# Stored sums instead of local ones for half 1 of a feed-forward product made with seven multiplications

## What is computed

```python
h = _rmsnorm(x, ln2_w[l])
u = jax.nn.relu(jnp.einsum("bsd,df->bsf", h, w_ff1[l]))
x = x + jnp.einsum("bsf,fd->bsd", jnp.square(u), w_ff2[l])
```

## Time and profile before

| | us |
|---|---|
| median of 3 runs | 1502.23 (1501.88 to 1502.95) |
| the profiled execution | 1503.15 |
| its span (first to last instruction) | 1501.3 |
| PE busy in the span | 1494.2 |
| half 0: first product / second product | 178.8 / 162.4 |
| half 1: first product / second product, to the end | 178.3 / 166.4 |

### The profile page before, as it was taken

One profiled execution on the slowest core, in us unless ns is written; L12 is line 12 of the kernel. 1 busy time (PEld: TensorE's weight loads), 2 busy tenths in 40 slices (PEclk: granted clock), 3 DMA queues, 4 the chain that ended last, 5 costly groups with the idle time before them and its releaser, 6 DMA issues.

```text
span 1501.3 us, 19534 instructions
## 1 busy us (share of the span) xinstructions
PE 1494.2 (100%) x7450; PEld 1257.9 (84%) x7450; DVE 1143.3 (76%) x1362; ACT 811.1 (54%) x925; POOL 130.9 (9%) x169
## 2 busy tenths in 40 slices
PE   9999999999999999999999999999999999999999
PEld 7888888888888888888888888888888888888877
DVE  6877756878787877876666777778988566578978
ACT  6555444676664544544444544456655445466654
POOL 6000000000041100100000111110000111110000
PEclk9999999999999999999999999999999999999999
DMA  8878897745545444446799888766877656666874
GB/s 293 216 256 294 302 341 264 241 159 169 171 166 168 141 140 162 144 142 205 268 320 326 268 287 293 244 224 221 302 261 265 193 188 195 191 222 217 311 283 149
DMA packets 156889, 345.37 MB, mean 230 GB/s; under 512 B 8336, under 2 KB 8848, under 8 KB 153488
## 3 DMA queue, kind: packets, MB, share of 16 engines
q1 hardware_dynamic: 148960, 317.09, 62.9%
q0 software_dynamic: 6592, 25.17, 4.7%
q10 hardware_dynamic: 1264, 2.13, 0.4%
HBM read 317.11 MB, written 27.26 MB: 229 GB/s over the span
## 4 chain that ended last, share of the span: by engine, by line
PE 93%; DVE 3%; DMA 2%; ACT 0%; issue 0%; SPq 0%; ACTq 0%; DVEq 0%
PE banks L630 46%; PE banks L1006 16%; PE banks L1052 9%; PE banks L1009 8%; PE banks L1074 6%; DVE lo L2192 2%; DMA raw<-in_w_ff 2%; PE banks L646 1%; DVE t_sums L2223 1%; PE banks L903 1%; PE banks L912 1%; DMA raw<-w_sums 0%; PE banks L788 0%; PE banks L764 0%; PE banks L667 0%
## 5 line engine op out<-in xcount | busy, mean ns | idle before, releaser
L1574 DVE TENSOR_TENSOR lo<-raw,hi 128x1024 fp32r<-128x1024 f32 x383 | 472.0, 1237 | 251.1 <-ACT hi L1107 249.9
L1107 ACT ACTIVATE hi<-raw 128x1024 fp32r<-128x1024 f32 x383 | 404.5, 1059 | 444.0 <-PE banks L630 263.5
L630 PE MATMUL banks<-hi,st 128*128 128x512 f32 x1584 | 499.1, 396 | 0.0
L630 PEld LDWEIGHTS banks<-hi,st 128*128 128x128 f32 x1584 | 290.6, 189 | 55.8 <-DVE lo L1574 0.7
L1006 PE MATMUL banks<-st,hi 128*128 128x512 f32 x1024 | 321.6, 395 | 0.0
L630 PE MATMUL banks<-lo,st 128*128 128x512 f32 x792 | 309.4, 391 | 0.0
L1009 PEld LDWEIGHTS banks<-st,lo 128*128 128x128 f32 x1024 | 192.4, 188 | 45.4
L1524 ACT ACTIVATE hi<-raw 128x1024 fp32r<-128x1024 f32 x160 | 168.7, 1061 | 110.6 <-PE banks L1074 61.8
L2192 DVE TENSOR_TENSOR lo<-raw,hi 128x1024 fp32r<-128x1024 f32 x160 | 192.5, 1222 | 22.0 <-ACT hi L1524 16.9
L1009 PE MATMUL banks<-st,lo 128*128 128x256 f32 x1024 | 201.1, 278 | 0.0
L630 PEld LDWEIGHTS banks<-lo,st 128*128 128x128 f32 x792 | 149.2, 188 | 31.6
(11 more groups left out here) (311 smaller groups left out, 1650.4 us busy)
## 6 DMA issues: line engine op xcount, KB each, us to landing
raw<-in_w_ff SPq DMA_DIRECT2D x116, 1024.0 KB, 5.9
raw<-in_w_in SPq DMA_DIRECT2D x99, 1024.0 KB, 5.0
raw<-w_sums SPq DMA_DIRECT2D x24, 1024.0 KB, 5.1
raw<-in_w_out SPq DMA_DIRECT2D x16, 1024.0 KB, 7.7
early_sum<-in_w_ff SPq DMA_DIRECT2D x12, 1024.0 KB, 8.0
w_sums<-early_sum SPq DMA_DIRECT2D x12, 1024.0 KB, 9.5
late_sum<-in_w_ff POOLq DMA_DIRECT2D x12, 1024.0 KB, 7.2
w_sums<-late_sum POOLq DMA_DIRECT2D x12, 1024.0 KB, 5.8
```

The lines of the kernel that those rows point to most:

```text
L630: last = pe.matmul(acc[:, t], x_t, v[:, (i + more) % PIECES, kk, :], start=m == 0 and kk == 0 and a == 0, stop=m == n - 1 and kk == 1 and ...
L1107: act.activation(hi[:, (i + more) % PIECES], raw[:, i // 2 % RAW, 2 * (i % 2):2 * (i % 2) + 2, :], ACT.Copy)\
L1574: dve.tensor_tensor(lo[:, (i + more) % PIECES], raw[:, i // 2 % RAW, 2 * (i % 2):2 * (i % 2) + 2, :], hi[:, (i + more) % PIECES].bitcast(F ...
```

## The change

In half 1 no octet is local any more: 2 and 5 are stored too. `STORED_OCTETS` orders the sixteen stored octets anew: the first six are of half 1, then come the six of half 0 as before, then four of half 1. Eight steps are added, four octets with two steps each. They stand in `LAST_STEPS` at pieces 6, 12, 17, 25, 28, 36, 44 and 52 of half 1's first product, with buffers `last` at the places of `u_hi[1][5]` and `u_hi[1][6]`, which are written later. GpSimd moves them. SyncE and ScalarE get the waits that belong to this. TensorE's order is the same row for row.

```diff
-LOCAL = ((2, 5), (2, 5))
-STORED = ((0, 3, 6), (0, 3, 6))
+LOCAL = ((2, 5), ())
+STORED = ((0, 3, 6), (0, 2, 3, 5, 6))
...
-STORED_OCTETS = [(half, np_, o) for half in (1, 0) for np_ in range(2) for o in STORED[half]]
+STORED_OCTETS = [[(half, np_, o) for np_ in range(2) for o in STORED[half]] for half in range(2)]
+STORED_OCTETS = STORED_OCTETS[1][:6] + STORED_OCTETS[0] + STORED_OCTETS[1][6:]
...
+LAST_STEPS = [6, 12, 17, 25, 28, 36, 44, 52]
...
+        last = [sb(f"last_sum{n}", [P, 2, 2 * N], F32, (182, 196)[n]) for n in range(2)]
...
-                    if half == 0:
+                    if 2 * n >= EARLY_STEPS:
                         for b in range(2):
                             sp.wait_ge(ev[f"l_out{b}"], 16 * n + 16 - 8 * EARLY_STEPS)
...
-            for o in SEVENS[1]:
-                token_sums(1, o)
+
+            pool.wait_ge(piece_used, piece0(0) + HALF_PIECES[0] + PIECES)
+            sum_in(FIRST_STEPS)
+            sum_in(FIRST_STEPS + 1)
+            h = FIRST_STEPS
+            for g in range(OCTETS):
+                if g and g - 1 in SEVENS[1]:
+                    token_sums(1, g - 1)
+                while h < ALL_STEPS and LAST_STEPS[h - FIRST_STEPS] < 8 * g + 8:
+                    sum_out(h)
+                    if h + 2 < ALL_STEPS:
+                        sum_in(h + 2)
+                    h += 1
...
             def late_stored(half, b):
-                if half == 0:
-                    act.wait_ge(ev[f"l_out{b}"], 8 * LATE_STEPS)
+                act.wait_ge(ev[f"l_out{b}"], 8 * ((ALL_STEPS if half else FIRST_STEPS) - EARLY_STEPS))
...
                 def parts():
                     u = us[g % 2]
+                    if half and g == OCTETS - 3:
+                        late_stored(half, 0)
...
-                          None if half else lambda p, g=g: stored_sums(8 * (QF0 + g) + p))
+                          (lambda p, g=g: stored_sums(8 * g + p, last_now)) if half else
+                          lambda p, g=g: stored_sums(8 * (QF0 + g) + p))
```

More of the change, by code:

```diff
@@ L85 @@
 MORE_PIECES = HALF_PIECES[0] - 64
-STORED_OCTETS = [(half, np_, o) for half in (1, 0) for np_ in range(2) for o in STORED[half]]
+STORED_OCTETS = [[(half, np_, o) for np_ in range(2) for o in STORED[half]] for half in range(2)]
+STORED_OCTETS = STORED_OCTETS[1][:6] + STORED_OCTETS[0] + STORED_OCTETS[1][6:]
 SUM_STEPS = [20, 28, 36, 44, 51, 56, 61, 66, 71, 76, 81, 86, 227, 234, 240, 245, 251, 261, 268, 276, 284, 292, 300, 308]
+LAST_STEPS = [6, 12, 17, 25, 28, 36, 44, 52]
 EARLY_STEPS, MIX_STEPS = 12, 5
-LATE_STEPS = len(SUM_STEPS) - EARLY_STEPS
-STORED_SUMS = 3 * len(SUM_STEPS)
+FIRST_STEPS, ALL_STEPS = len(SUM_STEPS), len(SUM_STEPS) + len(LAST_STEPS)
+FIRST_LOCAL = 4 * 2 * len(LOCAL[0])
 HALF_TILES = [2 * sum(4 if o in stored else 2 for o in range(OCTETS)) for stored in STORED]
@@ L316, in sums_before @@
             before = 2 * len(LOCAL[0]) * half + len(LOCAL[half]) * np_ + LOCAL[half].index(o)
-            return STORED_SUMS + 4 * before
+            return 3 * (ALL_STEPS if half else FIRST_STEPS) + 4 * before
         def weight_sum(half, np_, o, n):
@@ L323, in summed, with made_before, last_now @@
         def summed(h):
-            return (early if h < EARLY_STEPS else late)[h % 2]
+            return (early if h < EARLY_STEPS else late if h < FIRST_STEPS else last)[h % 2]
+        def made_before(h):
+            return 3 * h + (FIRST_LOCAL if h >= FIRST_STEPS else 0)
         def sums_now(at, after):
             return [h for h, step in enumerate(SUM_STEPS) if step + after == at]
+        def last_now(at, after):
+            return [FIRST_STEPS + n for n, step in enumerate(LAST_STEPS) if step + after == at]
         def source(half, np_, o, n):
@@ L584, in sum_out @@
             def sum_out(h):
-                pool.wait_ge(ev["t_made"], 3 * h + 3)
+                pool.wait_ge(ev["t_made"], made_before(h) + 3)
                 pool.dma_start(w_sums[h // 2, :, :, h % 2, :], summed(h)[:].rearrange("p r (c n) -> p (r c) n", c=2))\
@@ L600, in _ @@
                         token_sums(0, o - 1)
-                if h < len(SUM_STEPS):
+                if h < FIRST_STEPS:
                     sum_out(h)
-                    if h + 2 < len(SUM_STEPS):
+                    if h + 2 < FIRST_STEPS:
                         sum_in(h + 2)
                     h += 1
-            for o in SEVENS[1]:
-                token_sums(1, o)
+            pool.wait_ge(piece_used, piece0(0) + HALF_PIECES[0] + PIECES)
[10 more added lines that the diff above has]
+                    h += 1
         @block.tensor
@@ L1495, in late_stored @@
             def late_stored(half, b):
-                if half == 0:
-                    act.wait_ge(ev[f"l_out{b}"], 8 * LATE_STEPS)
+                act.wait_ge(ev[f"l_out{b}"], 8 * ((ALL_STEPS if half else FIRST_STEPS) - EARLY_STEPS))
             def u_hi_step(half, g):
                 def plain():
-                    if g == OCTETS - 1:
+                    if half == 0 and g == OCTETS - 1:
                         late_stored(half, 0)
@@ L1636, in right_lo, with stored_sums @@
                 return step
-            def stored_sums(at):
-                for h in sums_now(at, 0):
+            def stored_sums(at, now=sums_now):
+                for h in now(at, 0):
                     b = summed(h)
@@ L1647, in stored_sums @@
                     dve.tensor_tensor(upper, b[:, :, N:2 * N], upper, ALU.subtract).then_inc(ev["t_made"], 1)
-                    dve.wait_ge(ev["t_made"], 3 * h + 1)
+                    dve.wait_ge(ev["t_made"], made_before(h) + 1)
                     dve.tensor_tensor(lower[:, N:2 * N], lower[:, N:2 * N], b[:, 0, 0:N], ALU.subtract)\
                         .then_inc(ev["t_made"], 1)
-                for h in sums_now(at, 1):
+                for h in now(at, 1):
                     lower = summed(h)[:, 1]
-                    dve.wait_ge(ev["t_made"], 3 * h + 2)
+                    dve.wait_ge(ev["t_made"], made_before(h) + 2)
                     dve.tensor_tensor(lower[:, 0:N], lower[:, 0:N], lower[:, N:2 * N], ALU.subtract)\
```

## The result

The changed kernel takes **1509.29 us** (median of 6 runs, 1508.14 to 1510.24); the kernel before, beside it, 1502.27 (6 runs, 1501.88 to 1502.95). The ratio is 1.0046, with a 95% interval of 1.0033 to 1.0058: 7.0 us slower, where 1.0 was forecast. The profiled execution took 1508.14 us, its span 1506.4, against 1503.15 and 1501.3.

The account below looks back on a forecast made before the run. The prediction took TensorE to bound the kernel. From the profiled 1503.15 us, - 1.8 + 0 + 2.8 gave 1504.15; for the median, 1502.23 + 1.0 = 1503.2 us, with a range of 1500.0 to 1506.3.

Parts of the forecast that it names:

- 0.19 for slower: Chance given to a measurably slower kernel, above 1505.2 us; no difference had 0.79, faster 0.02.
- VectorE's sums leave the path: Half 1's second product: sixteen local sums go from VectorE, removing three TensorE pauses, worth 1.8 us at most.
- at octet 2 nothing is lost: Half 1's second product before the change: claimed no TensorE loss at local octet 2 beyond what four pieces of lead hide.
- The eight steps are hidden: Half 1's first product: eight added steps, 20.7 us of VectorE, and their new waits cost 0, bounds 0 to 2 us.
- Four stored pairs, each with one late tile: Half 1's second product: tile 3 of each pair's second octet lands late, 0.7 us each, 2.8 us; chance 0.53.
- the 5.87 us allowed: Second octet of a stored pair: tile 3 landing within 5.87 us of its issue costs TensorE nothing.
- the second pair: Profile row of two loads issued 0.5 us apart, the second taking 6.9 us; used to estimate tile 3's landing.
- the slower rival: Half 1's stored pairs: loads too slow, landing at 7.0 us or more, total from 1505.2 us; chance 0.16.
- The loads fall behind: Stored pairs and plain octet behind: tile 3 lands at 7.8 us, 2.0 us a pair, 1508.5 us; chance 0.16.
- its part by a fixed rate: Milder form: stored pairs load at a fixed rate below demand; 372 GB/s costs 0.7 us a pair, 2.8 in all.
- The 385 GB/s over 19 us: Claimed demand of a stored pair in half 1's second product, 7.34 MB in 19.04 us, under the best slices' 395 to 410.
- The rate from the Trainium skill: Limit of about 358 GB/s: a stored pair takes 20.5 us, 1.46 over TensorE, 1506.2 us; a third of 0.16.

Follow-up runs that it names:

- pairing: The changed kernel with the sums dealt to tiles in order 0, 0, 1, 2, 2, 3, 3 in both halves; 1499.65 us, ratio 0.9978 to the kernel before.
- before_pairing: The kernel before the change with only the new dealing of sums to tiles (0, 0, 1, 2, 2, 3, 3); 1501.13 us, ratio 0.9987.
- one_pair: The changed kernel with half 1's octet 5 local again and octet 2 stored, four added steps instead of eight; 1504.95 us, ratio 1.0012 to the kernel before.
- steps_only: The changed kernel making the eight added steps' sums, while half 1's second product forms its sums locally as before; 1502.79 us, ratio 1.0000 to the kernel before.
- the repeat of after: The changed kernel itself, unaltered, measured again beside other runs on one chip; 1510.19 us, ratio 1.0047 to the kernel before.
- places: The changed kernel with tiles 2 and 3 of half 1's octets 3 and 6 in memory of their own, loaded an octet earlier; 1502.0 us, ratio 0.9994.
- pairing_again: The changed kernel with the new dealing (0, 0, 1, 2, 2, 3, 3) in both halves, measured a second time; 1499.82 us, ratio 0.9976 to the kernel before.
- hold3: The changed kernel with tile 3's load in half 1's octets 3 and 6 issued one piece (1.36 us) later; 1506.64 us, ratio 1.0025 to the kernel before.

## Why the prediction was wrong

It gave 1503.2 us, with 1500.0 to 1506.3, and 0.19 for slower. The time is 1509.29. Step by step:

- **VectorE's sums leave the path**, -1.8 us. Right in size: the three pauses are gone. With the late tiles out of the way too, the step is worth 1.6 us (`pairing` against `before_pairing`). The place was misread. Only the pause at 1389 us lies at octet 5, in the first column half; the two at 1439 and 1441 us lie at octet 2 of the second, so "at octet 2 nothing is lost" is wrong. The chain of before shows it: the pause ends at 1441.63, then come the rest of this octet and octet 3 (66 matmuls), plain 4, octets 5 and 6 (84) and plain 7. The cause is the same, late tiles ahead of t1. `one_pair` was expected to keep all the 1.8 us at octet 5, from the same misreading.

```profile
1423.48 8.82 DMA raw<-in_w_ff
1432.40 1.23 DVE t_sums L2223
...
1441.63 15.24 PE banks L1052 x66
1456.87 10.88 PE banks L1074 x48
1467.75 19.04 PE banks L1052 x84
1486.79 10.89 PE banks L1074 x48
```

- **The eight steps are hidden**, 0. Right: 178.30 us for the first product, and `steps_only` at a ratio of 1.0000. GpSimd's and ScalarE's new waits show nowhere in PE's time.
- **Four stored pairs, each with one late tile**, 4 x 0.7 us. The place, the cause, the engine that waits, the count and the 5.87 us allowed were right, to 0.02 us in 20 pauses (the prediction's own terms, 12.58 less 6.69, give 5.89). The size was not: 6.55 us for 2.8. The step that failed is "from the second pair the two of them need 0.5 + 6.9 = 7.4 us from the first issue, which gives 6.0 here". It supposes that two loads land at a fixed time after the first issue, so that a later second issue waits less. The runs showed another thing: tile 3, issued 1.36 us behind tile 2, takes 6.8 to 8.3 us, 2.7 us behind it 5.0 to 6.3. With half the bytes ahead most of tile 3 came 1.2 us sooner, but its last part, and so the landing, still at 6.8 to 7.1. So 1.36 us of distance bought nothing against 0.5 us (6.9), and about 1 us of each landing of more than 8 us goes with a packet of another queue that the sum didn't have. The nearest row in distance was the plain pair, 1.2 us apart and 7.8 us to landing. I set it aside because it wasn't `w_sums`, and gave it to the slower rival.
- **The rivals.** "The loads fall behind" came nearest, with a landing of 7.8 us (7.1 to 8.2 measured) and 2.0 us a pair, 1508.5 in all; the chance of 0.16 was too small for the one price that a row showed at this distance. But its reason, that the queue can't bring the bytes, is wrong, and so is its part by a fixed rate: `pairing` brings the same bytes for the same octets without a pause. The 385 GB/s over 19 us that I set against it were no demand either: `pairing` gets through these stretches at 347 to 352.
- **The rate from the Trainium skill** ("DMA: Bandwidth & Descriptors", "Specifications", about 358 GB/s) came to 1506.2 by the estimate. That is nearer than my sum, for another reason: the estimate took 385 GB/s as the demand. `pairing` stays under 358 over 20 us and loses nothing, so nothing here speaks against the figure over such a length; over 2.8 us the repeat of after had 407.
- **The clock** was not in the sum. I priced a pause at its length and 0.1 us; two of four pauses of 2.6 us cost about 1.7 us more.

## What to carry to other kernels

Where a ring has no depth, ask for each place when its last reader is done and when its next tile is first read, and price the load by the row with the nearest *distance to the load ahead*. A load has landed when its slowest part has, so take the longest such row too. Then look at the order of use: letting the two reads of a tile stand next to each other frees the first place sooner and spreads the loads, with the same bytes, and here turned +7.0 us into -2.2, and into -3.5 with half 0 dealt the same way. Work that leaves an engine off the path is worth only the pauses that it made, and the loads that take its place can cost more.

## What I had not expected of the hardware

A 1 MiB load of stored sums landed in 4.9 to 5.2 us where nothing stood close ahead of it, in 6.8 to 8.3 where it was issued 1.36 us behind another, and in 5.0 to 6.3 at 2.7 us. The distance to the one ahead isn't all: where four or more followed each other closely, as in `places` or at octet 0 of `pairing` (2.3 us apart, 8.2 and 8.4, behind a 1 MB store of the output), loads took as long or longer, and one pair of `pairing_again`, 2.7 us apart, took 7.4 and 7.2. Issued later, it can land earlier: in `hold3` tile 3 left 1.36 us later and landed, counted from tile 2's issue, at 9.0 us instead of after's 9.6 in that pair, and at 7.8 instead of 8.4 in the third. In one execution with half the bytes ahead, half of the load's sixteen last packets were through 1.2 us sooner, and still it landed only 0.3 to 1.2 us sooner, with the last of the sixteen. What makes that one late is open. And TensorE, at 2.4 GHz in the rest of the stage, was found at 1.2 GHz for some 3.5 us after two pauses of 2.6 us, and not after two others.
